# Norms of a one-core streaming-encoder layer taken token tile by token tile: order of the output product, roots, scalings and transposes

## What is computed

```python
def rms_norm(x, g):
    r = lax.rsqrt(jnp.mean(xf * xf, axis=-1, keepdims=True) + EPS)
    return (xf * r * g).astype(x.dtype)

h = rms_norm(x, g_mix)
z = h @ w_in                                   # pool | q | k | v | two gates
merged = sigmoid(gate_pool) * y_pool + sigmoid(gate_attn) * y_attn
x = x + merged @ w_out
x = x + peer_layer(rms_norm(x, g_ffn), w_peer_q, keys_1, keys_2, expert_down, expert_up)
return rms_norm(x, g_final)
```

## Time and profile before

| | us |
|---|---|
| median of 3 runs | 3030.55 (3023.52 to 3033.89) |
| profiled execution, its own time | 3019.19 |
| span of its trace | 3017.4 |
| PE busy in the span | 2844.6 (94%) |
| DVE, POOL, ACT busy | 2336.3, 2124.3, 937.1 |

### The profile page before, as it was taken

How to read it: one execution, slowest core, us unless ns; L and a number is a source line. 1 busy time by engine, 2 the same in 40 slices (tenths; PEclk the granted TensorE clock), 3 DMA queues, 4 the chain that set the end, 5 groups by cost and what they waited for, 6 DMA issues and landing times.

```text
span 3017.4 us, 40171 instructions
## 1 busy us (share of the span) xinstructions
PE 2844.6 (94%) x15235; PEld 2477.6 (82%) x15235; DVE 2336.3 (77%) x4348; ACT 937.1 (31%) x1356; POOL 2124.3 (70%) x1552
## 2 busy tenths in 40 slices
PE   7999898999899799899999998999999989999996
PEld 6678777677689688889998997899899979989995
DVE  1332298345499899588999999898899979889998
ACT  4232433232332399322222222222222222222221
POOL 4324576338568799778887886888688868878883
PEclk9899999899899899999999999999999999999998
DMA  3112412112322377989998997999899979989996
GB/s 140 43 63 91 168 64 70 42 50 98 112 87 94 120 238 237 332 310 330 347 349 315 342 336 289 335 342 341 311 343 336 346 266 339 348 311 341 335 337 219
DMA packets 267584, 717.92 MB, mean 238 GB/s; under 512 B 20864, under 2 KB 104064, under 8 KB 267392
## 3 DMA queue, kind: packets, MB, share of 16 engines
q0 software_dynamic: 110912, 403.75, 35.8%
q1 hardware_dynamic: 156480, 311.61, 30.6%
HBM read 657.86 MB, written 57.41 MB: 237 GB/s over the span
## 4 chain that ended last, share of the span: by engine, by line
PE 34%; DVE 8%; POOL 7%; DMA 6%; issue 3%; ACT 1%; DVEq 0%; SPq 0%; ACTq 0%
PE abank L1530 6%; PE abank L1532 6%; PE abank L1531 6%; PE ybank L1546 6%; PE ybank L1547 5%; PE ybank L1548 5%; POOL up L1475 3%; DVE acc L1684 3%; DMA up<-in_down,e_idx 3%; POOL tdown_lo L1482 2%; DMA up<-in_up,e_idx 2%; DVE up L1672 2%; DVE e_y L1731 1%; POOL tup_lo L1486 1%; DMA w<-all_pre 1%
## 5 line engine op out<-in xcount | busy, mean ns | idle before, releaser
L1530 PE MATMUL abank<-m_hT,tdown_hi 128*128 128x384 f32 (+1 forms) x1856 | 576.4, 311 | 15.0 <-ACT w L1588 9.0
L817 POOL TENSOR_TENSOR m_wlo<-m_raw,m_whi 128x1024 fp32r<-128x1024 f32 x128 | 309.5, 2425 | 379.9 <-ACT m_whi L622 376.7
L1532 PE MATMUL abank<-m_hT,tdown_lo 128*128 128x384 f32 (+1 forms) x1856 | 575.9, 310 | 0.0
L1531 PE MATMUL abank<-m_hlo,tdown_hi 128*128 128x384 f32 (+1 forms) x1856 | 574.9, 310 | 0.0
L1546 PE MATMUL ybank<-tup_hi,w_hi 128*128 128x512 f32 x1280 | 509.1, 398 | 45.5 <-DVE e_y L1731 32.7
L1684 DVE SCALAR_TENSOR_TENSOR acc<-up,e_act,acc 128x1024 f32<-128x1024 f32 x381 | 489.7, 1285 | 65.9 <-DMA up<-in_up,e_idx 43.4
L1672 DVE CUSTOM_DVE_ANT_0 up<-up,acc 128x1024 f32<-128x1024 f32 x384 | 457.0, 1215 | 97.8 <-DMA up<-in_down,e_idx 95.2
L1547 PE MATMUL ybank<-tup_lo,w_hi 128*128 128x512 f32 x1280 | 506.2, 396 | 0.0
L1548 PE MATMUL ybank<-tup_hi,w_lo 128*128 128x512 f32 x1280 | 504.2, 394 | 0.0
L1475 POOL DMA_INDIRECT up<-in_up,e_idx x384 | 396.9, 1033 | 106.0 <-issue 92.4
L1475 POOL DMA_INDIRECT up<-in_down,e_idx x384 | 399.1, 1039 | 99.3 <-issue 88.9
(11 more groups left out here) (226 smaller groups left out, 4714.6 us busy)
## 6 DMA issues: line engine op xcount, KB each, us to landing
e_tup<-in_up SPq DMA_DIRECT2D x128, 512.0 KB
m_raw<-in_tiles SPq DMA_DIRECT2D x116, 512.0 KB, 3.3
e_tdown<-in_downT SPq DMA_DIRECT2D x116, 512.0 KB
gates<-all_table SPq DMA_DIRECT2D x64, 640.0 KB
all_table<-t_out SPq DMA_DIRECT2D x9, 4096.0 KB, 14.7
m_raw<-in_downT SPq DMA_DIRECT2D x12, 512.0 KB, 3.7
up<-in_down,e_idx POOLq DMA_INDIRECT x384
up<-in_up,e_idx POOLq DMA_INDIRECT x384
```

Source lines behind the costliest of these rows:

```text
L1530: nc.tensor.matmul(out, tdown_hi[:, q, at], h2T_hi[:, k, a:b], start=k == 0, stop=False)
L1531: nc.tensor.matmul(out, tdown_hi[:, q, at], h2T_lo[:, a:b, at], start=False, stop=False)
L1532: ins = nc.tensor.matmul(out, tdown_lo[:, q, at], h2T_hi[:, k, a:b], start=False, stop=k == KD - 1)
```

## The change

- **Output product.** `SPLIT_OUT = KD - RING = 5`. For k = 0 to 4 nothing changes. The last three weight tiles (5, 6, 7) are taken per token tile: for t = 0, 1, 2 each bank (t, n) gets k = 5, 6, 7 in a row and is then handed over; t = 3 takes k = 5, 6, 7 with both banks inside, and releases weight tiles 5 and 6 as it goes.
- **Norm (g, 1)** goes tile by tile: squares, variance, root and the five small steps for each t alone. Scaling: tiles 0 and 1 on DVE, tile 2 on ACT, tile 3 half on ACT and half on DVE. ACT splits `pq` 0 between the root and the scaling of tile 2, and `pq` 1 and `pq` 2 after the scaling of tile 3.
- **Norm (0, 0)** goes by pairs of tiles; scaling: 0 on DVE, 1 on POOL, 2 on ACT, 3 on DVE.
- **Norm (1, 0)** keeps one root; ACT scales tile t after key score 12 + t, into other places (`junk`).
- **Transposes** go token tile by token tile over all eight banks; a bank is handed over after tile 3.
- **A one-element Sqrt** (`sqrt_soon`) at the start and before norm (g, 1) loads ACT's table ahead of need.
- POOL and SP keep their order; h is counted by the engine that scaled it.

```diff
+ROOTS = {norm: ((0,), (1,), (2,), (3,)) for norm in NORMS}
+ROOTS[0, 0] = ((0, 1), (2, 3))
+ROOTS[1, 0] = ((0, 1, 2, 3),)
+SCALES = {norm: ("dve", "dve", "act", "both") for norm in NORMS}
+SCALES[0, 0] = ("dve", "pool", "act", "dve")
+SCALES[1, 0] = ("act", "act", "act", "act")
+SPLIT_OUT = KD - RING
...
-                pe.wait_ge(h_ready, g * 2 * TT + TT)
-                for k in range(KD):
-                    turn(("xT", k), [h[:, t, k * P:(k + 1) * P] for t in range(TT)])
+                def turn_normed(name, n):
+                    for t in range(TT):
+                        wait_scaled(pe, g, n, t)
+                        for k in range(KD):
+                            out = begin(name, k) if t == 0 else bank(name, k)
+                            ins = nc.tensor.transpose(out[:, t * P:(t + 1) * P], scaled_place(g, n, t)[:, k * P:(k + 1) * P], ident)
+                            if t == TT - 1:
+                                ins.then_inc(job_full, 1)
+                turn_normed("xT", 0)
...
+                for k in range(SPLIT_OUT):
                     pe.wait_ge(m_low, g * KD + k + 1)
-                    for t, n in outs:
...
+                    for t in range(TT):
+                        for n in range(2):
+                            ins = out_term(k, t, n)
+                    ins.then_inc(out_used, 1)
+                pe.wait_ge(m_low, g * KD + KD)
+                for t in range(TT - 1):
+                    for n in range(2):
+                        for k in range(SPLIT_OUT, KD):
+                            ins = out_term(k, t, n)
+                        ins.then_inc(job_full, 1)
+                for k in range(SPLIT_OUT, KD):
+                    for n in range(2):
+                        ins = out_term(k, TT - 1, n)
                         if k == KD - 1:
                             ins.then_inc(job_full, 1)
                     if k < KD - 1:
                         ins.then_inc(out_used, 1)
-                pe.wait_ge(h_ready, g * 2 * TT + 2 * TT)
-                for k in range(KD):
-                    turn(("xT2", k), [h[:, t, k * P:(k + 1) * P] for t in range(TT)])
+                turn_normed("xT2", 1)
...
-            root(0, 0)
-            scaled(0, 0)
+            act.wait_ge(x_in[0], 16)
+            sqrt_soon(x[:, 0, 0:1])
+            for of in ROOTS[0, 0]:
+                for t in of:
+                    act.wait_ge(x_in[t], 16)
+                    ins = squares(t, h[:, t])
+                ins.then_inc(ssq_ready, 1)
+                root(0, 0, of)
+            scaled(0, 0, 2)
             tile_high(1)
...
-                for k in range(KD - 1):
+                for k in range(SPLIT_OUT):
                     after("out", k)
                     if g and k == 3:
                         gates_exp(g - 1)
+                sqrt_soon(vecs[:, 0:1])
                 for t in range(TT):
                     act.wait_ge(x2_ready, g * 2 * TT + 2 * t + 2)
-                    ins = squares(t, h[:, t])
-                ins.then_inc(ssq_ready, 1)
-                after("out", KD - 1)
-                root(g, 1)
-                scaled(g, 1)
+                    squares(t, h[:, t]).then_inc(ssq_ready, 1)
+                    root(g, 1, (t,))
+                    if t == 2:
+                        after("out", SPLIT_OUT)
+                        scaled(g, 1, 2)
+                scaled(g, 1, 3)
+                for k in range(SPLIT_OUT + 1, KD):
+                    after("out", k)
                 turned(g, 1)
...
+                    if more and n >= 12:
+                        scaled(g + 1, 0, n - 12)
...
                 if more:
-                    scaled(g + 1, 0)
                     turned(g + 1, 0)
...
+            pool.wait_ge(rinv_ready, roots_until(0, 0, 1))
+            nc.gpsimd.tensor_scalar(h[:, 1], x[:, 1], rinv[:, 1:2], None, ALU.mult).then_inc(h_by["pool"], 1)
...
+                def finish_norm(t):
+                    norm_end(g, 1, (t,))
+                    if SCALES[g, 1][t] != "act":
+                        scaled(g, 1, t)
                 for t in range(TT):
+                    if t:
+                        finish_norm(t - 1)
                     for n in range(2):
                         wait_job(dve, g, "xo", t, n)
                         part = x[:, t, n * 512:(n + 1) * 512]
                         nc.vector.tensor_tensor(part, part, bank("xo", t, n)[:], ALU.add).then_inc(x2_ready, 1)
-                norm_start(g, 1)
-                norm_end(g, 1)
+                    norm_start(g, 1, (t,))
+                finish_norm(TT - 1)
```

More of the change, by code:

```diff
@@ L113, with roots_until, scales_until @@
 JOBS = mixer_jobs()
+NORMS = [(g, n) for g in range(NG) for n in range(2)]
+ROOTS = {norm: ((0,), (1,), (2,), (3,)) for norm in NORMS}
[4 more added lines that the diff above has]
+SCALES[1, 0] = ("act", "act", "act", "act")
+def roots_until(g, n, t):
+    before = sum(len(ROOTS[norm]) for norm in NORMS[:NORMS.index((g, n))])
+    return before + [t in of for of in ROOTS[g, n]].index(True) + 1
+def scales_until(engine, g, n, t):
+    of = [who for norm in NORMS[:NORMS.index((g, n))] for who in SCALES[norm]] + list(SCALES[g, n][:t + 1])
+    return sum(who == engine or who == "both" and engine != "pool" for who in of)
+SPLIT_OUT = KD - RING
 NJ = len(JOBS)
@@ L258, in mixer @@
         rinv_ready = sem("rinv_ready")
-        h_ready = sem("h_ready")
+        h_by = {engine: sem(f"h_by_{engine}") for engine in ("act", "dve", "pool")}
         hT_ready, hT_low = sem("hT_ready"), sem("hT_low")
@@ L911, in _ @@
                     pool.wait_ge(late_in, 16 * 3)
-                    pool.wait_ge(h_ready, 2 * TT)
+                    for t in range(TT):
+                        wait_scaled(pool, g, 1, t)
                     pool.wait_ge(x2_out, 16 * TT)
```

86 lines of the change are left out of this document (54 added, 32 removed).

## The result

The changed kernel took 3030.76 us (median of 20 runs, 3021.34 to 3035.64), the kernel before 3023.51 beside it (20 runs, 3016.66 to 3033.89). The ratio is 1.0022, 95% interval 1.0014 to 1.0029: **some 6.7 us slower, where the forecast was 1.4 faster** (7.25 between the medians). The three runs known at the prediction had given 3030.55 for the kernel before, so the absolute time of 3029.0 came near by luck; the comparison side by side is what counts. It is inside the 0.3% that I had called no change, but with the wrong sign. The profiled execution took 3030.24, its span 3028.4 against 3017.4. The trace of the kernel before is that of an execution of 3019.19, 4.3 under its median here, so the 11.0 between the two spans overstates the change.

A forecast was written before the change was run, and what follows sets the result against it. PE bounded the kernel, idle 42.1 us in four waits for the scaled x. Terms -4.4 + 3.3 - 0.3 + 0 = -1.4 took the median 3030.55 to 3029.1, said as 3029.0 us, range 3019 to 3037.

The forecast's parts named there:

- Start: Norm (0, 0): table load ahead and scaling by pairs let projection 1 start at 24.4 instead of 28.75 us, -4.4.
- Ring gap, group 0: Output product, group 0: PE stands 2.4 us idle for weight tile 7, and the lower clock costs 1.8 more.
- Chain per tile: Norm (0, 1): each token tile takes 5.0 us through DVE and ACT, against 4.2 of PE's matmuls.
- Late stores: Behind norm (0, 1): stores issued 15 us later; PE stands 6.7 before the fourth query projection, which ends 8 later.
- Choice: Group 0 after norm (0, 1): most lateness absorbed, ACT's squares for norm (1, 0) pass on about 4; +3.3 us.
- (c): Slower: the stall of PE at `pq` 3 passes through the choice whole; +9, 3039.6 us, chance 0.07.
- Norm (1, 0): At norm (1, 0): two of four scalings move ahead of PE's end; -0.3 us, between -1.2 and +1.4.
- Group 1: Output product and norm (1, 1): PE 4.6 us late for weight tiles, 1.8 of clock; 0, or -1.9 if clock holds.
- (a): In the choice, POOL's lateness is absorbed and DVE starts 1.0 earlier and keeps it; -6.7, 3023.9 us, chance 0.20.
- (b): Output product, both groups: neither ring gap hurts, clock stays up, no POOL cost; -11, 3019.5 us, chance 0.11.
- (d): Norm (0, 0): POOL's one scaling blocks DVE's first scaling and variance; -2 instead of -4.4, 3031.5 us, chance 0.05.

The follow-up runs named there:

- e11: Changed kernel with POOL's choice of head 0 ahead of the low part of `pq` 8 and ACT's squares one key score earlier; 3026.98 us, ratio 1.0005.
- e7: Changed kernel with POOL's choice of head 0 in group 0 put ahead of the low part of `pq` 8; 3027.34 us, ratio 1.0008.
- e3: Changed kernel without the split of the output product, `pq` 0 and 1 split ahead of the norm's end; 3020.33 us, ratio 0.9974.
- e9: The same kernel as e3, run again in more rounds; 3020.84 us, ratio 0.9987.
- e1: Changed kernel with the stores of the new x issued one tile earlier, ahead of the load of `pq` 4; 3024.04 us, ratio 0.9992.
- e2: Kernel before with its stores of x in group 0 held until the second low part of norm (0, 1); 3034.95 us, ratio 1.0020.

## Why the prediction was wrong

- **Start:** right, -3.7 for -4.4 in this trace and 4 in the mean of all. The forecast chain of causes up to weight tile 1 is in the rows.
- **Ring gap, group 0:** right (2.24 idle and about 1.6 of clock, for 2.4 and 1.8). Chain per tile 4.56 for 5.0. First query result -0.6 for -1.0. The cost of the gap is not certain, though: e11 has the same 2.24 idle and lost no clock (last section).
- **Late stores:** right up to PE's stall. 5.86 idle for 6.7, and the fourth query result 8.2 late for 8.
- **Choice:** the step that failed is "What passes it on is ACT's squares for norm (1, 0)". The squares' end was foreseen well (423.3 less the start's 3.7 is 419.6; measured 419.4), and e7 shows that they would have held DVE, and that the price would have been right: with POOL's choice ahead, the first low part of norm (1, 0) is 3.5 later than before, the start set aside, for a forecast of 3.3 - 0.3 = 3.0 (PE's stall was 9.5 there, with 8 in the forecast). But POOL's choice of head 0 held DVE first, for 4.08 until 410.23, so that it came to the variances only at 420.84, behind the squares, and there POOL's next operation held the step for 2.37. Rival (c) named this: it "decides once POOL's first choice ... is more than 3 behind DVE's hits". I gave it 0.07 without working out when that choice would end, though all its terms stood in the trace. By the forecast's own clock the fourth query result comes at 384.4; two more at 6.47 make 397.3; ACT's split of `pq` 8 and POOL's low part add 4.2; the choice takes 12.2: 413.7, or 410.0 with the start's 3.7 off. Measured: 410.1, 4.1 after DVE wanted it. The term was **+7.4 for +3.3**.
- A second slip in the same step: I measured the lateness of the squares against the end of the variance step, 419.47, which before was itself held 2.2 by POOL. Against its start, 417.11, the squares are 6 late, not 4. The 4 stands only if the step is then not held, as in e7 (0.22); in the changed kernel it was (2.37).
- **Norm (1, 0):** +0.5 for -0.3, inside its bounds. PE starts 3.0 sooner behind the last result, as worked out, and the last tile undoes it.
- **Group 1:** +0.2 for 0. Two waits, 3.56 and 0.69, for one of 4.6. This is one reading of a stretch whose repeats differ by 2.5 (e3, e9).
- **The rivals:** (c) gave the right mechanism with too high a price: +9 at the mixer's end, where +4.4 came. Its terms were 8 for the stall, 2.6 for group 1, -3 for the start and 1.4 for norm (1, 0), and 7.4, 0.2, -3.7 and 0.5 were measured. (a) failed: e1 shows what it would have taken, no stall. (b) failed, as both ring gaps stood, and (d), as the start gained. Of the 6.7 by the ratio the mixer's mark explains 4.4, or 8.1 from `out` 7; neither is good to better than 2 or 3, so whether anything behind the mixer adds to it stays open.
- Of the signs that the prediction named, projection 1 at 24.4, the idle PE with clock 0.5 at the split, h ready less the start's gain (342.8; it was 341.4) and PE's idle time ahead of the fourth query projection are there; the stores are 10.1 later, 13.8 with the start's gain set against it, for 15; DVE's wait for ACT's squares is there only in e7.
- e1 and e2 show that the late stores are the loss, and e7 and e11 how it is passed on.

## What to carry to other kernels

When a step moves, follow every queue behind it to the first place where two engines take turns, and work out there which of them comes last; a wait that was hidden by 2 us may be the one that passes everything on, and the next one may stand right behind it. Finishing tiles early is worth having only if the loads and stores queued on the same engines do not move back with it: here storing one tile earlier took the loss away, and leaving out the split made the kernel faster than both. Measure a part alone before it is built into the rest: the split alone cost 0.6%, and all the rest without it gained 0.1 to 0.3%, most of which the marks put at the very first norm. And count from a mark ahead of the edit: traces of the same code differed by up to 3.5 us there.

## What the runs showed of the hardware

The same idle time does not always cost the clock. In e11 the split's gap is that of the changed kernel, 2.24, but PE went on at a granted clock of 1.00 (2.4 GHz), where the changed kernel had 0.51:

```profile
317.92 0.50 PE L479 MATMUL bank<-m_whi,m_mhi 128*128 128x512 f32 x1 [2.24 <-POOL m_wlo L893]
```

```profile
318.00:322.00 4.00, 4.00 (x18) 3.28 (x19) 1.38 (x2) 0.27 (x1) 0.00 (x0) 1.00 0.42 131
```

In group 1, PE waits for POOL in front of output block 3; e3 and e9, the same kernel, first e3 (its matmul behind the gap, and the window behind it), then e9:

```profile
770.03 0.47 PE L479 MATMUL bank<-m_whi,m_mhi 128*128 128x512 f32 x1 [3.30 <-POOL m_wlo L881]
```

```profile
770.00:775.00 5.00, 4.96 (x22) 4.11 (x23) 2.71 (x3) 0.00 (x0) 5.00 (x2) 1.00 0.61 212
```

```profile
770.72 0.76 PE L479 MATMUL bank<-m_whi,m_mhi 128*128 128x512 f32 x1 [3.54 <-POOL m_wlo L881]
```

```profile
770.00:775.00 5.00, 4.29 (x10) 3.45 (x11) 3.07 (x3) 0.27 (x1) 5.00 (x3) 0.50 0.53 155
```

After 3.30 idle PE went on at a clock of 1.00 (2.4 GHz), after 3.54 at 0.50 (1.2 GHz) over the whole window, which is most of the 2.5 between the two traces. So a gap of 2 to 4 us costs either nothing or about 2 more, and one trace can't settle a difference of 2.

Loading ACT's table ahead costs only the load: in the changed kernel it starts at 317.37 and the next activation at its end, 1.29 later.

```profile
317.37 1.28 ACT L703 ACT_TABLE_LOAD   x1
318.66 0.20 ACT L703 ACTIVATE m_small<-m_vecs 128x1 f32<-128x1 f32 x1
```
